# Output projections by Strassen's seven half products, in blocks of 512 tokens, on one Trainium2 core

## The chip, the cores and the metric

The kernel runs as one program on one core of a Trainium2 chip. The metric is the device time of one execution in microseconds (us); the time before is 4362.51 us, the median of 3 runs that lie between 4362.19 and 4364.94 us. Engines are named as in the profile: PE is the matrix engine (PEld its weight loads), DVE the vector engine, ACT the scalar engine, POOL the GpSimd engine, SP the sync engine, which here issues DMAs.

## The reference

Two blocks of a network over 1024 latent tokens of width 1024, with 256 context tokens beside them. The part that the change touches is the projection by which each of three mixers ends. All is in float32.

```python
def mixer(h, hc, ...):                 # first block, one layer
    ...
    y_lat = jnp.concatenate([hy_lat, gla_lat, gdn_lat], axis=-1) @ w_out
    ...
# first_block:  x = x + g1 * y
#               x = x + g2 * sq_relu_mlp(modulate(x, norm2_g[l], sh2, sc2), w_mlp1[l], w_mlp2[l])

def hybrid_layer(x, ctx, ...):         # second block, two layers
    ...
    out_x = jnp.concatenate([att_x, m_x], axis=-1) @ w_out
    x = x + gate_x * out_x
    if not last:
        ...
        out_c = jnp.concatenate([att_c, m_c], axis=-1) @ w_out
        ctx = ctx + gate_c * out_c
    return x, ctx
# between them and at the end: rmsnorm over the width
```

Each `w_out` is 1024 x 1024.

## The kernel before

Activations lie transposed in on-chip memory: the width is split into 8 tiles of 128 partitions, tokens run along the free dimension. Tokens are worked in the blocks of `BLKS` (L17): 512, 512 and, where the context is alive, 256. A plan (`plan`, L4193) yields stages; each stage is an object with a method for each engine, which writes that engine's instructions in order. Nothing reorders them afterwards: an engine's queue is the order of the stages and, within one, the order of its loops. Engines meet by semaphores only: `then_inc` at the producer, `wait_ge` at the consumer; `Stage.begin` (L242) lets an engine wait for all engines' last step of the stage named `after`.

`OutProj` (L2627) is the stage of the change. It stands in the plan three times: "one" (L4244, two blocks), "two0" (L4280, three blocks, the third is the context) and "two1" (the same line, two blocks). In `tensor` (L2645) it goes through the blocks i and in each through the 8 output tiles j. An output tile is 8 float32 matmuls (one for each input tile k) of a 128 x 128 weight against the block's tokens, summed in one of six PSUM banks. The profile counts each float32 matmul as two MATMUL instructions. Weights come in four slots of 256 output columns (`Weights`, L172; `sync`, L2636), each loaded once and used by all blocks. `vector` (L2672) first waits for the whole of x to be back from DRAM, then adds each output tile times its gate to x (L2679). `scalar` (L2663) squares the new x (L555, `Sums.square`), `gpsimd` (L2684) adds the squares up (L565, `Sums.add`) for the norm that follows. x comes back by one DMA that `RestoreX` (L2612) puts on POOL's queue just ahead of `OutProj`; it waits for the end of the stage before.

From block 1 on, each method also issues, behind tile j, a part j of the stage that follows (`post`) for block i-1, so that the norm of block 0 is worked while block 1 is projected. For "one" and "two0" that is `Rms` (L647): PE sums the squares over partitions at j=1 (L572, L574), ACT makes Ln and Exp of it at j=2 (L723, L725), DVE scales (L709) two tiles each at j=3, 4 and 5 and one each at j=6 and 7, and ACT shifts each scaled tile (L729), waiting for it. For "two1" it is `Finish` (L2818): at j=2 to 5 PE transposes 128 tokens into banks 6 and 7 (L2854), and ACT and DVE scale them out of these banks.

Of the kernel before, what the change touches and what calls it, by code (L numbers as in the profile page):

```python
# [9 lines left out]
ALU = mybir.AluOpType  # L10
# [3 lines left out]
T, TC, TT = 1024, 256, 1280  # L14
D = 1024
NEG = -1.0e30
BLKS = [(0, 512), (512, 512), (1024, 256)]  # L17
# [350 lines left out]
class Modulation(Stage):  # L368
# [14 lines left out]
    def steps(self, one, turn):  # L383

        held = None
        for j in self.js:
            one(j)
            if held is not None and self.many:
                turn(held)
            held = j  # L390
            yield
            if not self.many:
                turn(j)
                held = None
            for _ in range(self.gap):
                yield
        if held is not None:
            turn(held)
# [1526 lines left out]
class GlaScan(Stage):  # L1925
# [45 lines left out]
    def four(self, x, t0):  # L1971

        return x[:, :, t0:t0 + 256].rearrange("p a (c t) -> p a c t", c=2)
# [653 lines left out]
class OutProj(Stage):  # L2627

    def __init__(self, K, tag, w, gates, blks, after, sums, post, away=None):
        super().__init__(K, "out_proj", tag, after)
        self.w, self.gates, self.blks, self.sums, self.post, self.away = w, gates, blks, sums, post, away
        self.cat = K.big[:, K.M0:K.M0 + 8 * (TT if len(blks) == 3 or tag != "one" else T)]

    def sync(self, e):  # L2636
        for j in range(0, 8, 2):
            self.K.W.put_cols(e, self.w, 128 * j, 256)

    def steps(self):  # L2640
        for i, (t0, n) in enumerate(self.blks):
            for j in range(8):
                yield i, t0, n, j, (self.tag, "out", j, t0)

    def tensor(self, e):  # L2645
        K, P = self.K, self.sig("tensor")
        self.begin(e)
        pr = Banks(K, range(6))
        cat = self.cat.rearrange("p (a b) -> p a b", a=8)
        ws = []  # L2650
        for i, t0, n, j, u in self.steps():
            if i == 0 and j % 2 == 0:
                ws.append(K.W.use(e, 256))
            used, wv = ws[j // 2]
            b = pr.open(e, u)
            for k in range(8):
                c = 128 * (j % 2)
                t = e.matmul(b[:, 0:n], wv[:, k, c:c + 128], cat[:, k, t0:t0 + n], start=(k == 0), stop=(k == 7))  # L2658
            t.then_inc(P.sem, P.up(("mm", u), used))
            if i:  # L2660
                self.post.tensor_part(e, i - 1, j)

    def scalar(self, e):  # L2663
        S = self.sig("scalar")
        self.begin(e)
        for i, t0, n, j, u in self.steps():
            e.wait_ge(*self.at("free", u, 0))
            self.sums.square(e, S, i, j)
            if i:
                self.post.scalar_part(e, i - 1, j)  # L2670

    def vector(self, e):  # L2672
        K, V = self.K, self.sig("vector")
        self.begin(e)
        e.wait_ge(*self.at("x back", self.tag))
        for i, t0, n, j, u in self.steps():
            x = K.XT[:, j, t0:t0 + n]
            e.wait_ge(*self.at("mm", u))
            e.scalar_tensor_tensor(x, self.bank(u)[:, 0:n], self.gates[1 if t0 >= T else 0][:, j:j + 1], x, ALU.mult,  # L2679
                                   ALU.add).then_inc(V.sem, V.up(("free", u, 0)))  # L2680
            if i:
                self.post.vector_part(e, i - 1, j)

    def gpsimd(self, e):  # L2684
        K, G = self.K, self.sig("gpsimd")
        self.begin(e)
        for i, t0, n, j, u in self.steps():
            self.sums.add(e, G, i, j)
            if i:
                self.post.gpsimd_part(e, i - 1, j)  # L2690
            if self.away is not None and i == len(self.blks) - 1:
                X = self.lane(f"x{j}_away")
                e.wait_ge(*self.at("free", u, 0))
                e.dma_start(K.xs[:, j, :], K.XT[:, j, :]).then_inc(X.sem, X.up(("x away", self.away, j), by=16))


class Mlp(Stage):
# [1495 lines left out]
def plan(K):  # L4193

    A = K.A
    yield Setup(K, "setup", "setup")
    yield Close(K, "setup")
    tmp = K.spare()
    sums = Sums(K, "rms1", K.XT, BLKS, tmp, tmp)
# [7 lines left out]
    m = GdnMem(K)  # L4207
# [6 lines left out]
    m = GlaMem(K)  # L4214
# [8 lines left out]
    m = HyMem(K)  # L4223
# [20 lines left out]
    yield OutProj(K, "one", A["w_out"][0], (K.m6(2), None), BLKS[0:2], "hyena", sums, rms)  # L4244
    yield rms
    yield load
    yield Close(K, "rms2")
# [10 lines left out]
    for l in range(2):  # L4258
        md = K.adac[:, l, :, :]
        m = MlMem(K)  # L4260
# [16 lines left out]
        else:  # L4277
            post = Finish(K, sums, A["final_g_2"])
            yield Fetch(K, post)
        yield OutProj(K, f"two{l}", A["p_out"][l], (md[:, 16:24, 0], md[:, 16:24, 1]), blks, f"at{l}", sums, post,  # L4280
                      "ml1" if l == 0 else None)
        yield post
        yield Close(K, f"rms{5 + l}")

# [96 lines left out]
```

## Time and profile before

| | |
|---|---|
| time, median of 3 | 4362.51 us (4362.19 to 4364.94) |
| span of the profiled execution | 4364.0 us |
| PE busy | 4013.5 us, 92% |
| DVE, ACT, POOL busy | 1530.0, 944.2, 577.8 us |
| mean granted PE clock | 0.949 of full speed |
| DMA | 64 GB/s mean |
| chain that ended last | PE 85%, DVE 7%, issue 3%, ACT 2%, DMA 2%, POOL 1% |
| share of L2658 (the projections' matmuls) in that chain | 8% |

The time of this profiled execution outside its span is not recorded; its span lies 1.5 us above the median of the timed runs. In a row of a line's group, "xcount | busy, mean ns | idle before, releaser" gives how often an instruction ran, its summed time, its mean duration and how long the engine had stood idle before it. Matmuls overlap in the pipeline, so the mean duration of one is longer than its pace; the pace is read from stretches. The granted clock is 1.00 at 2.4 GHz and 0.50 at 1.2 GHz.

### The profile page before, as it was taken

To read this page: it belongs to the slowest core of one execution; us is meant where nothing else is said; L and a number is where in the kernel's file an instruction comes from. 1 tells how busy PE (TensorE), PEld (TensorE's weight loads), DVE (VectorE), ACT (ScalarE), POOL (GpSimd) and SP (SyncE) were. 2 spreads that over 40 slices of the span, in tenths; PEclk is the share of its full clock that TensorE was granted. 3 is DMA by queue.
4 is the path that set the end of the run, shared out by engine and by line. 5 is a ranking of instruction groups with operands and counts; after the bars stand their busy time and mean duration, and the time that the engine had idled before them with its cause. 6 is when DMAs were issued, how large, how long until landed. Compare 5 with 4: busy or idle time off the path is not lost.

```text
span 4364.0 us, 51611 instructions
## 1 busy us (share of the span) xinstructions
PE 4013.5 (92%) x21278; PEld 2527.3 (58%) x21278; DVE 1530.0 (35%) x3530; ACT 944.2 (22%) x1814; POOL 577.8 (13%) x603
## 2 busy tenths in 40 slices
PE   5897997988999999999999897899989998799899
PEld 3477995576467444444444456885554557775454
DVE  2573553235444101111113644531162363621341
ACT  4122331222100200000002411320252310320341
POOL 3002331023000110000002201211000101201001
PEclk7996998988999999999999999999999999999999
DMA  5201002035345111111110312211100312211100
GB/s 189 102 5 26 25 25 88 25 104 180 101 156 203 39 39 39 39 39 39 37 36 28 125 30 73 73 40 51 54 1 25 140 36 57 76 59 39 44 25 39
DMA packets 215480, 278.17 MB, mean 64 GB/s; under 512 B 24333, under 2 KB 174056, under 8 KB 214352
## 3 DMA queue, kind: packets, MB, share of 16 engines
q1 hardware_dynamic: 201904, 206.17, 15.1%
q0 software_dynamic: 13344, 68.70, 4.2%
q8 instruction: 171, 2.80, 0.3%
q14 instruction: 61, 0.50, 0.0%
HBM read 240.03 MB, written 34.81 MB: 63 GB/s over the span
## 4 chain that ended last, share of the span: by engine, by line
PE 85%; DVE 7%; issue 3%; ACT 2%; DMA 2%; POOL 1%; SPq 0%; POOLq 0%; DVEq 0%; ACTq 0%
PE ps L805 16%; PE ps L2748 10%; PE ps L2762 10%; PE ps L2658 8%; PE ps L827 7%; PE ps L3417 6%; PE ps L3699 4%; PE ps L2419 3%; PE ps L3910 2%; PE ps L3893 1%; PE ps L851 1%; DVE big L3512 1%; PE ps L1475 1%; PE ps L1459 1%; DMA big<-hs_scratch 1%
## 5 line engine op out<-in xcount | busy, mean ns | idle before, releaser
L805 PE MATMUL ps<-big 128*128 128x512 f32 (+1 forms) x1760 | 685.6, 551 | 2.8 <-DMA big<-hs_scratch 2.8
L805 PEld LDWEIGHTS ps<-big 128*128 128x128 f32 x1760 | 335.6, 192 | 343.7 <-issue 334.4
L2748 PE MATMUL ps<-big 128*128 128x512 f32 x1024 | 442.3, 594 | 8.6 <-issue 8.6
L2762 PE MATMUL ps<-big 128*128 128x512 f32 x1024 | 440.8, 592 | 0.0
L2812 DVE SCALAR_TENSOR_TENSOR big<-ps,big 128x512 f32<-128x512 f32 x128 | 96.0, 750 | 776.8 <-PE ps L2762 776.8
L2658 PE MATMUL ps<-big 128*128 128x512 f32 (+1 forms) x896 | 359.3, 562 | 3.0 <-DVE big L4028 2.0
L2748 PEld LDWEIGHTS ps<-big 128*128 128x128 f32 x1024 | 195.1, 191 | 254.2 <-issue 254.2
L2762 PEld LDWEIGHTS ps<-big 128*128 128x128 f32 x1024 | 194.6, 190 | 244.9 <-issue 244.9
L827 PE MATMUL ps<-big 128*128 128x256 f32 (+1 forms) x1792 | 319.2, 341 | 12.5 <-DVE big L1909 10.1
L827 PEld LDWEIGHTS ps<-big 128*128 128x128 f32 x1792 | 288.3, 194 | 43.9 <-DVE big L1909 10.3
L2658 PEld LDWEIGHTS ps<-big 128*128 128x128 f32 x896 | 169.6, 190 | 187.6 <-issue 180.8
L3417 PE MATMUL ps<-big 128*128 128x256 f32 x1152 | 251.9, 380 | 5.9 <-DVE big L3590 3.3
L3417 PEld LDWEIGHTS ps<-big 128*128 128x128 f32 x1152 | 217.8, 190 | 36.1 <-issue 6.8
L2779 ACT ACTIVATE big<-ps 128x512 f32<-128x512 f32 x64 | 38.2, 597 | 725.6 <-PE ps L2748 725.6
L932 DVE SCALAR_TENSOR_TENSOR big<-big 128x1024 f32<-128x1024 f32 x130 | 167.0, 1285 | 4.6
L3699 PE MATMUL ps<-big 128*128 128x512 f32 (+1 forms) x416 | 164.7, 552 | 1.9 <-DVE big L3590 1.9
L565 POOL TENSOR_TENSOR big<-big 128x512 f32<-128x512 f32 (+1 forms) x90 | 108.9, 1215 | 403.7 <-ACT big L555 401.5
L2796 POOL TENSOR_TENSOR big<-big 128x512 f32<-128x512 f32 x64 | 66.5, 1039 | 698.0 <-ACT big L2779 698.0
L555 ACT ACTIVATE big<-big 128x512 f32<-128x512 f32 (+1 forms) x120 | 68.7, 595 | 406.3 <-DVE big L2679 310.3
L2679 DVE SCALAR_TENSOR_TENSOR big<-ps,big 128x512 f32<-128x512 f32 (+1 forms) x56 | 39.8, 712 | 311.9 <-PE ps L2658 293.3
L3699 PEld LDWEIGHTS ps<-big 128*128 128x128 f32 x416 | 80.1, 193 | 83.0 <-issue 78.3
L3403 PE MATMUL ps<-big 128*128 128x129 f32 x288 | 63.8, 306 | 69.8 <-DVE big L3526 63.6
(458 smaller groups left out, 5256.4 us busy)
## 6 DMA issues: line engine op xcount, KB each, us to landing
big<-in_w_mlp SPq DMA_DIRECT2D x32, 1024.0 KB, 5.4
big<-in_w_in SPq DMA_DIRECT2D x29, 1024.0 KB, 5.2
big<-in_w_mod SPq DMA_DIRECT2D x24, 1024.0 KB, 5.3
big<-in_w_ada SPq DMA_DIRECT2D x24, 1024.0 KB, 6.3
big<-us_scratch SPq DMA_DIRECT2D x72, 256.0 KB, 4.4
hs_scratch<-big POOLq DMA_DIRECT2D x3, 5120.0 KB, 16.8
big<-c_dft SPq DMA_DIRECT2D x12, 1024.0 KB, 5.7
xs_scratch<-big POOLq DMA_DIRECT2D x16, 640.0 KB, 3.5
```

The lines of the kernel that those rows point to most:

```text
L565: e.tensor_tensor(self.acc[i], self.acc[i], self.sq[q % len(self.sq)][:, 0:n], ALU.add).then_inc(G.sem, G.up(("added", self.tag, q), ("sum ...
L805: t = e.matmul(b[:, 0:n], wv[:, k, 128 * m:128 * m + 128], K.hT[:, k, t0:t0 + n], start=(k == 0), stop=(k == 7))
L827: t = e.matmul(b[:, 0:nn], K.hT[:, k, 128 * i:128 * i + 128], wv[:, k, 0:nn], start=(k == 0), stop=(k == 7))
L932: e.scalar_tensor_tensor(dlat, zlat[:, :, tap:tap + c.seg], c.wcol(m, tap), dlat, ALU.mult, ALU.add).then_inc(V.sem, V.up((self.tag, c.wha ...
L2419: x = e.matmul(b[:, 0:ncol], v[:, t, 128 * k:128 * k + 128], src[:, 4 * half + t, :], start=(t == 0), stop=(t == 3))
L2658: t = e.matmul(b[:, 0:n], wv[:, k, c:c + 128], cat[:, k, t0:t0 + n], start=(k == 0), stop=(k == 7))
L2748: t = e.matmul(b[:, :], wv[:, k, 128 * m:128 * m + 128], K.hT[:, k, t0:t0 + n], start=(k == 0), stop=(k == 7))
L2762: t = e.matmul(b[:, :], wv[:, k, 128 * m:128 * m + 128], h[:, k, t0:t0 + n], start=(k == 0), stop=(k == 3))
L2812: e.scalar_tensor_tensor(x, self.bank(u)[:, :], self.gcol[:, c:c + 1], x, ALU.mult, ALU.add).then_inc(V.sem, V.up(("free", u, 0)))
L3417: x = e.matmul(b[:, 256 * q:256 * q + 256], m.hT[:, k, 128 * t:128 * t + 128], wv[:, k, :], start=(k == 0), stop=(k == 7))
L3699: t = e.matmul(b[:, 0:n], wv[:, k, c:c + 128], K.hT[:, k, t0:t0 + n], start=(k == 0), stop=(k == 7))
L3910: t = e.matmul(self.o[64 * g:64 * g + 64, :], self.m.vtm[:, tiles[k][1], 64 * g:64 * g + 64], tile[g], start=(k == 0), stop=(k == len(tile ...
```

## The change

In `OutProj`, for blocks 0 and 1 (512 tokens), each weight slot (256 output columns, p = 0 to 3) is cut into four quarters W[i][j] (output half i of 128 columns, input half j of four tiles), the block's input into X[j][l] (input half j, token half l of 256 tokens). The direct method makes the 2 x 2 result by eight quarter products; the change makes it by seven, each of 4 float32 matmuls over 256 tokens. For that POOL makes four combinations of the weight quarters for each slot, in block 0, DVE makes four combinations of the input quarters once a block, and intermediate sums are read out of PSUM on the way: DVE adds 7 results of 256 tokens for each slot in place of 2 of 512. Three PSUM results a, b and d are held for each slot; a takes four products one after the other, and before the next is added, DVE must have read it ("P1 out", "P16 out", "P167 out"; for d "P5 out"). One of the weight combinations is written over a weight quarter, so the context block (third block of "two0"), which stays direct (`whole`), has its weights loaded again. The three input combinations that have memory of their own (T1, T2, T4) are shared by the blocks; the fourth is written over the input.

```diff
+    def seven(self, e, P, pr, i, used, wv, p):
+        W, X, (S1, S2, S4), (T1, T2, T4) = self.weights(wv), self.inputs(i), self.S[p], self.T
+        a, b, d = self.unit(i, p)
+        def product(u, w, x, first):
+            o = self.bank(u)[:, 0:256]
+            for k in range(4):
+                t = e.matmul(o, w[:, k, :], x[:, k, :], start=(first and k == 0), stop=(k == 3),
+                             skip_group_check=not first)
+            return t
+        pr.open(e, a)
+        product(a, W[0][0], X[0][0], True).then_inc(P.sem, P.up(("P1", a)))
+        pr.open(e, b)
+        product(b, W[0][1], X[1][0], True).then_inc(P.sem, P.up(("mm", b)))
+        e.wait_ge(*self.at(self.tag, "weight sum", p, 2))
+        e.wait_ge(*self.at(self.tag, "input sum", i, 2))
+        e.wait_ge(*self.at("P1 out", a))
+        product(a, S2, T2, False).then_inc(P.sem, P.up(("P16", a)))
+        pr.open(e, d)
+        product(d, S1, T1, True).then_inc(P.sem, P.up(("P5", d)))
+        e.wait_ge(*self.at(self.tag, "weight sum", p, 3))
+        e.wait_ge(*self.at(self.tag, "input sum", i, 3))
+        e.wait_ge(*self.at("P16 out", a))
+        product(a, W[1][0], X[0][1], False).then_inc(P.sem, P.up(("P167", a)))
+        e.wait_ge(*self.at(self.tag, "weight sum", p, 4))
+        e.wait_ge(*self.at("P5 out", d))
+        product(d, S4, X[1][1], False).then_inc(P.sem, P.up(("mm", d)))
+        e.wait_ge(*self.at(self.tag, "input sum", i, 4))
+        e.wait_ge(*self.at("P167 out", a))
+        product(a, W[1][1], T4, False).then_inc(P.sem, P.up(("mm", a), used, (self.tag, "block", i)))
     def tensor(self, e):
...
+        for i in range(len(self.blks)):
+            for p in range(4):
+                if i != 1:
+                    ws.append(K.W.use(e, 256))
+                (self.whole if i == 2 else self.seven)(e, P, pr, i, *ws[4 * (i == 2) + p], p)
+                if i:
+                    for j in (2 * p, 2 * p + 1):
+                        self.post.tensor_part(e, i - 1, j)
     def scalar(self, e):
...
+        for i in range(len(self.blks)):
+            for j in range(8):
+                e.wait_ge(*self.at(self.tag, "x", i, j))
+                self.sums.square(e, S, i, j)
+                if i:
+                    self.post.scalar_part(e, i - 1, j)
+    def input_sums(self, e, V, i):
+        X, (T1, T2, T4) = self.inputs(i), self.T
+        if i:
+            e.wait_ge(*self.at(self.tag, "block", i - 1))
+        e.tensor_tensor(T1, X[0][1], X[0][0], ALU.subtract).then_inc(V.sem, V.up())
+        e.wait_ge(V.sem, V.n)
+        e.tensor_tensor(T2, X[1][1], T1, ALU.subtract).then_inc(V.sem, V.up((self.tag, "input sum", i, 2)))
...
     def vector(self, e):
...
+        for i, (t0, n) in enumerate(self.blks):
+            if i < 2:
+                self.input_sums(e, V, i)
+            if i == 0:
+                e.wait_ge(*self.at("x back", self.tag))
+            for p in range(4):
...
+                    add(i, a, ("P1", a), j, t0, 256, ("P1 out", a))
+                    add(i, b, ("mm", b), j, t0, 256, ("free", b, 0))
+                    add(i, a, ("P16", a), j, t0 + 256, 256, ("P16 out", a))
+                    add(i, d, ("P5", d), j + 1, t0 + 256, 256, ("P5 out", d))
+                    add(i, a, ("P167", a), j + 1, t0 + 256, 256, ("P167 out", a))
+                    add(i, d, ("mm", d), j, t0 + 256, 256, ("free", d, 0), (self.tag, "x", i, j))
+                    add(i, a, ("mm", a), j + 1, t0, 256, ("free", a, 0), (self.tag, "x", i, j + 1))
+                if i:
+                    for x in (j, j + 1):
+                        self.post.vector_part(e, i - 1, x)
+    def weight_sums(self, e, G, p):
...
+        e.tensor_tensor(S1, W[1][0], W[1][1], ALU.add).then_inc(G.sem, G.up())
+        e.wait_ge(G.sem, G.n)
+        e.tensor_tensor(S2, S1, W[0][0], ALU.subtract).then_inc(G.sem, G.up((self.tag, "weight sum", p, 2)))
+        e.tensor_tensor(W[1][0], W[0][0], W[1][0], ALU.subtract).then_inc(
+            G.sem, G.up((self.tag, "weight sum", p, 3)))
+        e.wait_ge(*self.at(self.tag, "weight sum", p, 2))
+        e.tensor_tensor(S4, W[0][1], S2, ALU.subtract).then_inc(G.sem, G.up((self.tag, "weight sum", p, 4)))
     def gpsimd(self, e):
...
+        for i in range(len(self.blks)):
+            for j in range(8):
+                if i == 0 and j % 2 == 0:
+                    self.weight_sums(e, G, j // 2)
+                self.sums.add(e, G, i, j)
```

`Sums.add` does nothing for j = 0 and 7; for the others it waits for the square of tile j.

## Rows read from the trace of the kernel before

**Rows 1.** The page: busy time of the engines, and the group of L2658.
```profile
PE 4013.5 (92%) x21278; PEld 2527.3 (58%) x21278; DVE 1530.0 (35%) x3530; ACT 944.2 (22%) x1814; POOL 577.8 (13%) x603
...
L2658 PE MATMUL ps<-big 128*128 128x512 f32 (+1 forms) x896 | 359.3, 562 | 3.0 <-DVE big L4028 2.0
```
**Rows 2.** The chain that ended last: start us, us, what.
```profile
1391.97 68.91 PE ps L2658 x160
...
3310.97 68.91 PE ps L2658 x160
...
3431.42 20.73 PE ps L2658 x96
...
4232.77 68.91 PE ps L2658 x160
```
**Rows 3.** Timeline of DVE, the first add of each stage (start us, us).
```profile
1406.15 1.41 DVE L2679 SCALAR_TENSOR_TENSOR big<-ps,big 128x512 f32<-128x512 f32 x2 [16.62 <-PE ps L2658]
...
3320.54 0.75 DVE L2679 SCALAR_TENSOR_TENSOR big<-ps,big 128x512 f32<-128x512 f32 x1 [9.78 <-DMA big<-xs_scratch]
...
4241.26 0.75 DVE L2679 SCALAR_TENSOR_TENSOR big<-ps,big 128x512 f32<-128x512 f32 x1 [8.70 <-DMA big<-xs_scratch]
```
**Rows 4.** L2679 by duration (ns min/median/max), and three groups of DVE by form.
```profile
L2679 DVE SCALAR_TENSOR_TENSOR big<-ps,big x56: 483/750/752, 1406.2 to 4348.2; 128x512 f32<-128x512 f32 x48, 128x256 f32<-128x256 f32 x8
...
L932 DVE SCALAR_TENSOR_TENSOR big<-big 128x1024 f32<-128x1024 f32 x130 | 167.0, 1285 | 4.6
...
L709 DVE SCALAR_TENSOR_TENSOR big<-big 128x512 f32<-128x512 f32 x64 | 50.0, 832 | 20.6 <-ACT big L725 20.6
...
L3748 DVE TENSOR_TENSOR big<-big 128x512 f32<-128x512 f32 x20 | 13.9, 693 | 14.5 <-POOL big L3667 14.5
```
**Rows 5.** Timelines of ACT and POOL, start of stage "one": square, then add.
```profile
1413.64 0.63 ACT L555 ACTIVATE big<-big 128x512 f32<-128x512 f32 x1 [5.42 <-DVE big L2679]
...
1414.35 1.26 POOL L565 TENSOR_TENSOR big<-big 128x512 f32<-128x512 f32 x1 [4.70 <-ACT big L555]
```
**Rows 6.** POOL's sums of two tiles: min/median/max ns of L565 and L2796.
```profile
L565 POOL TENSOR_TENSOR big<-big x90: 713/1266/1723, 28.4 to 4342.8; 128x512 f32<-128x512 f32 x72, 128x256 f32<-128x256 f32 x18
...
L2796 POOL TENSOR_TENSOR big<-big x64: 1038/1039/1040, 1526.3 to 2288.4; 128x512 f32<-128x512 f32 x64
```
**Rows 7.** Timeline of ACT and DVE in block 1 of stage "one".
```profile
1470.94 1.28 ACT L723 ACT_TABLE_LOAD   x1
...
1474.23 0.63 ACT L725 ACTIVATE big<-big 128x512 f32<-128x512 f32 x1
...
1483.90 1.41 DVE L709 SCALAR_TENSOR_TENSOR big<-big 128x512 f32<-128x512 f32 x2
```
**Rows 8.** Timeline of PE behind three stretches of idleness.
```profile
1516.77 28.45 PE L2748 MATMUL ps<-big 128*128 128x512 f32 x62 [8.60 <-issue]
...
2405.71 2.08 PE L572 MATMUL ps<-big 128*128 128x512 f32 x2 [4.73 <-ACT big L734]
...
2950.01 15.67 PE L3699 MATMUL ps<-big 128*128 128x512 f32 x32 [0.94 <-DVE big L3590]
```
**Rows 9.** Windows behind them: stretch, busy of each engine, PEclk, DMA, GB/s.
```profile
1519.00:1520.00 1.00, 1.00 (x2) 0.34 (x1) 0.00 (x0) 0.17 (x2) 0.72 (x1) 0.50 0.00 0
...
2410.00:2411.00 1.00, 1.00 (x3) 0.39 (x2) 0.29 (x1) 0.00 (x0) 0.00 (x0) 0.55 0.00 0
...
2952.00:2953.00 1.00, 1.00 (x2) 0.34 (x2) 0.00 (x0) 0.00 (x0) 0.80 (x3) 0.50 0.50 168
```
**Rows 10.** Timeline of PE in stage "two1", block 1: transposes for `Finish`.
```profile
4310.17 1.04 PE L2854 MATMUL ps<-big 128*128 128x128 f32 x8
```
**Rows 11.** Timelines at the end of stages "one" and "two0": ACT and PE.
```profile
1505.28 0.72 ACT L729 ACTIVATE big<-big 128x512 f32<-128x512 f32 x1
...
1505.31 1.12 PE L574 MATMUL ps<-big 128*128 128x512 f32 x2 [0.65 <-ACT big L555]
...
3453.16 0.70 PE L574 MATMUL ps<-big 128*128 128x256 f32 x2 [0.59 <-ACT big L555]
```

More of the change, by code:

```diff
@@ L2636, in sync, with weights @@
     def sync(self, e):
[L2637 to L2643, printed above, removed]
+        for _ in range(len(self.blks) - 1):
+            for j in range(0, 8, 2):
+                self.K.W.put_cols(e, self.w, 128 * j, 256)
+    def weights(self, wv):
+        return [[wv[:, 4 * j:4 * j + 4, 128 * i:128 * i + 128] for j in range(2)] for i in range(2)]
@@ new lines, in inputs, with places, four @@
+    def inputs(self, i):
+        t0 = self.blks[i][0]
+        return [[self.cat[:, 4 * j:4 * j + 4, t0 + 256 * l:t0 + 256 * l + 256] for l in range(2)] for j in range(2)]
+    @staticmethod
+    def places(K, mem, last):
+        def four(x):
+            return x.rearrange("p (k c) -> p k c", k=4)
+        T, S = [mem.get(4, 256) for _ in range(2)], [four(K.columns().get(512)), four(mem.get(512))]
+        if last:
+            S += [four(K.R1[:, 4096 + 512 * i:4608 + 512 * i]) for i in range(8)]
+            return T + [mem.get(4, 256)], S + [four(mem.get(512)), four(K.R1[:, 9224:9736])]
+        S += [four(K.hT0[:, k, 512:1024]) for k in range(8)]
+        S += [K.hT0[:, 4:8, 1024 + 128 * j:1152 + 128 * j] for j in range(2)]
+        return T + [K.hT0[:, 0:4, 1024:1280]], S
@@ new lines, in unit, with whole @@
+    def unit(self, i, p):
+        return [(self.tag, "out", i, p, x) for x in "abd"]
+    def whole(self, e, P, pr, i, used, wv, p):
+        t0, n = self.blks[i]
+        for m in range(2):
+            u = (self.tag, "out", i, 2 * p + m)
+            b = pr.open(e, u)
+            for k in range(8):
+                t = e.matmul(b[:, 0:n], wv[:, k, 128 * m:128 * m + 128], self.cat[:, k, t0:t0 + n], start=(k == 0),
+                             stop=(k == 7))
+            t.then_inc(P.sem, P.up(("mm", u), used))
@@ L2648, in tensor @@
         pr = Banks(K, range(6))
[L2649 to L2661, printed above, removed]
+        self.base, ws = K.W.uses, []
+        for i in range(len(self.blks)):
[6 more added lines that the diff above has]
+                        self.post.tensor_part(e, i - 1, j)
     def scalar(self, e):
@@ new lines, in vector @@
+        for i, (t0, n) in enumerate(self.blks):
[4 more added lines that the diff above has]
+            for p in range(4):
+                j = 2 * p
+                if i == 2:
+                    for m in range(2):
+                        u = (self.tag, "out", i, j + m)
+                        add(i, u, ("mm", u), j + m, t0, n, ("free", u, 0), (self.tag, "x", i, j + m))
+                else:
+                    a, b, d = self.unit(i, p)
+                    add(i, a, ("P1", a), j, t0, 256, ("P1 out", a))
[8 more added lines that the diff above has]
+                        self.post.vector_part(e, i - 1, x)
@@ L2686, in gpsimd @@
         self.begin(e)
[L2687 to L2694, printed above, removed]
+        for i in range(len(self.blks)):
[3 more added lines that the diff above has]
+                self.sums.add(e, G, i, j)
+                if i:
+                    self.post.gpsimd_part(e, i - 1, j)
+                if self.away is not None and i == len(self.blks) - 1:
+                    X = self.lane(f"x{j}_away")
+                    e.wait_ge(*self.at(self.tag, "x", i, j))
+                    e.dma_start(K.xs[:, j, :], K.XT[:, j, :]).then_inc(X.sem, X.up(("x away", self.away, j), by=16))
 class Mlp(Stage):
@@ L4243, in plan @@
     rms = Rms(K, "rms2", K.XT, K.hT0, BLKS[0:2], [(sums, i) for i in range(2)], tmp, cols, begun=1)
-    yield OutProj(K, "one", A["w_out"][0], (K.m6(2), None), BLKS[0:2], "hyena", sums, rms)
+    mem = OutProj.places(K, tmp, 0)
+    yield OutProj(K, "one", A["w_out"][0], (K.m6(2), None), BLKS[0:2], "hyena", sums, rms, mem)
     yield rms
```

31 lines of the change are left out of this document (17 added, 14 removed).

## The prediction

> **What bounds the kernel now.** I read the page first: PE is busy 92% of the span, and the projections' matmuls (L2658) are 359.3 us of it, with 3.0 us of idleness ahead of them in all [rows 1]. Then the chain that ended last: in each of the three stages it is PE alone, 160 MATMULs in 68.91 us without a break [rows 2]. So PE's pace is the stage's time, nothing else shows, and a saved matmul is a gain as long as nothing new makes PE wait. The pace is 68.91 / 160 = 430.7 ns for 512 columns and 20.73 / 96 = 215.9 ns for 256 columns, each with its own weights [rows 2]: half the columns cost almost exactly half, so the smaller products lose nothing by themselves. Last I read what the other engines do in these stages, since the change makes PE wait for them inside each slot: today six banks keep PE apart from them, and DVE's first add comes 14.18, 9.57 and 8.49 us after the stage's first matmul (first row of each stage in [rows 2] against [rows 3]) without PE noticing.
>
> **What is removed.** A weight slot ("pair" of output tiles) in a block of 512 is now 32 MATMULs of 512 columns, 32 x 0.4307 = 13.78 us. After: 7 products x 4 x 2 = 56 of 256 columns, 56 x 0.2159 = 12.09 us. That is 1.69 us for each of 24 pairs (four pairs, two blocks, three stages), 40.6 us in all. The context block keeps its matmuls; its second load of 4 MB follows slots that come free a block earlier, and I cost it at nothing: three pairs of context, 3/4 x 20.73 = 15.5 us of PE, hide even the last slot [rows 2].
>
> **What is added: waits of PE.** The first two products need nothing; they end 3.45 us into the pair. The third needs the weight sum S2, the input sum T2 and "P1 out", DVE's add of the first product. The five products from there on take 8.64 us. So a pair costs 8.64 us plus the time at which the last of the three is there, at least 3.45. DVE's add of 256 columns is 0.48 us [rows 4]. Later waits in the pair each have a whole product (8 x 0.2159 = 1.73 us) for one add and hold nobody up.
>
> *Block 0, first pair.* DVE waits for all of x before "P1 out", so it is there at 14.18, 9.57 and 8.49 us plus 0.48: 14.66, 10.05, 8.97. Behind that wait stand all of DVE's adds, and now PE. The four input sums stand ahead of it and are hidden by it (about 5 us, below). The pairs take 23.3, 18.7 and 17.6 us in place of 13.78: +9.5, +4.9, +3.8, together **+18.2**.
>
> *The clock.* PE now stands idle 11.2, 6.6 and 5.5 us there. In the trace, after 8.60 us of idleness 62 MATMULs took 28.45 us in place of 26.7 and the granted clock was still 0.50 at 1519; after 4.73 us it was 0.55 in the window at 2410, 5 us after the restart at 2405.71; behind light work with short gaps 32 MATMULs took 15.67 us in place of 13.78 [rows 8, 9]. The losses are 1.75, about 2.6 and 1.9 us. I take 1.9 three times, **+5.7**; bounds 0 to 2.6 each.
>
> *Block 0, pairs 2 to 4.* POOL comes to the weight sums of a pair only behind the sum of squares of the last tile but one of the pair before (L565), since `gpsimd` is written so. From the end E of a pair: DVE's add until 0.52 (0.04 to start), the square 0.63 from there (1.17), POOL starts 0.08 later [rows 5] and does the square's sum, S1 and S2, three instructions of 1.26 us [rows 5, 6]: S2 at E + 5.03, pair 13.67 us, -0.11 for each of nine pairs, **-1.0**. The gain of these pairs is eaten by POOL. The weight sums' own form is not in the trace: bounds are 1.04 us (L2796) and 1.72 us (the longest L565, beside DVE work on SBUF); I take 1.26, the median of the form nearest to it [rows 6].
>
> *Block 1, first pair.* T1, T2 and T4 are shared with block 0, so DVE starts the four input sums only when block 0's last product is done, and its own add of that product and the add of P1 lie around them. A sum of 128 x 1024 from SBUF is not in the trace: twice 0.693 less one start-up as the lower bound, 1.285 (L932) as the upper one [rows 4]; I take 1.24. P1 out at 0.52 + 4 x 1.24 + 0.48 = 5.96, pair 14.6 us: +0.86 three times, **+2.6**.
> The Trainium skill (VectorE: DVE Perf Modes, the cycle table with its errata) gives a float32 sum of two tensors (N + 151) / 0.96 ns, an estimate of 1.22 us here; the whole sum would change by 0.3 us.
>
> *Block 1, pair 2.* Nothing new: -1.69 three times, **-5.1**.
>
> *Block 1, pairs 3 and 4 under `Rms`.* The parts for both tiles now stand behind all seven adds. In pair 2 ACT makes Ln and Exp with their table loads, 1470.94 to 1474.86, 3.9 us [rows 7]; it starts behind the square of tile 2, whose last product ends 1.73 before E and whose add ends at E - 1.21, so at E - 0.55, and is done at E + 3.4. DVE then scales two tiles (1.41 us, [rows 7]) and only then reads P1: 3.4 + 1.41 + 0.48 = 5.3, pair 13.9: +0.16. In the next pair DVE has four tiles to scale, 0.70 to 0.83 us each [rows 4, 7], I take 3.1 us: 0.52 + 3.1 + 0.48 = 4.1, pair 12.74: -1.04. For two stages: **-1.8**.
>
> *Block 1, pairs 3 and 4 in "two1".* `Finish` has PE transpose twice behind a pair, each 8 MATMULs, 1.04 us in all [rows 10], into the same two banks; the second now has no tile of matmuls between and waits for ACT and DVE (0.75 us) to empty them, some 0.45 us. Two times -1.69 + 0.45: **-2.5**.
>
> *Ends.* The last square stood 0.8 us behind the last matmul. Now ACT's shift of tile 6 is ahead of it in ACT's queue, and that waits for DVE's scaling of tile 6, which stands behind the last add: add until 0.52, scaling until 1.25, shift (0.72) until 2.0, square until 2.65, against 1.5 at which L574 starts today [rows 11]. **+1.2** in "one", +1.3 in "two0" (its L574 follows 1.2 behind), -0.3 in "two1", which has no such part: together **+2.2**.
>
> **The sum.** 18.2 + 5.7 - 1.0 + 2.6 - 5.1 - 1.8 - 2.5 + 2.2 = +18.3 us. Said the other way: a gross gain of 40.6 against 59 us of new waits, 23.3 of them for x, 5.7 of clock, 30 for sums, norms and ends. On the profiled span 4364.0 + 18.3 = 4382.3; what lies around the span is not touched, and the median of the runs stands 1.5 us lower: **4381 us**.
>
> **Rivals.** *A, cheap waits.* POOL's three instructions run at 1.04 us, as L2796 does with both inputs the same, and the clock stays up in "two0" and "two1": 9 x 0.66 + 3.8 = 9.7 us less, 4371. Against it: L565 has two inputs and a median of 1.27 us [rows 6].
> *B, contention and clock.* POOL's weight sums run at 1.72 beside DVE, 9 x 2 x 0.45 = +8, and every second of the twelve short stops of 1.6 to 2.5 us lets the clock fall as the stretch at 2950 did (1.9 us [rows 8, 9]), +11: 4389 to 4400. For it: that stretch had no stop longer than 2 us. Against it: PE works at full load between the stops here.
> The Trainium skill (TensorE: Matmul & The Clock Gate, "A second HAM failure mode: psum-queue depth-cycling") says that small idle times between groups of matmuls alone can make the clock go up and down; it speaks for this rival, and against the change.
> *C, faster.* Only the wait for x is left as a stop. Its place is the third product of each pair: if from the second pair on S2 and P1 out are there by 3.45 us, POOL's chain of 5.03 us would have to shrink by 1.6 and DVE would have to be free of sums and scalings by then. Then the gain is 40.6 - 23.3 - 5.7 = 11.6, 4351 us. It decides in favour of the change as soon as the 30 us behind the first pairs fall under 11.6. No row shows POOL or DVE at such a pace.
> *D, the seven products don't run in 7/8 of the time.* Each wait splits PE's stream into groups of 8 MATMULs, and where PE really stops, one MATMUL's pace (0.22 us) may be lost to the weight load that can't be hidden: 21 stops, up to +4, 4385.
>
> **Chances.** Forecast 0.60; A 0.14; B 0.15; C 0.05; D 0.06. The range leaves out C and the far end of B: **4367 to 4396**. A change of 0.2% (8.7 us, 4353.8 to 4371.2) is about what a measurement of this kernel can tell from none. Faster than that: C, 0.05. Within it: half of A and the low tail of the forecast, 0.13. Slower: 0.82.
>
> **What would show it.** Right: in the changed kernel's timeline PE stands still about 11, 6.6 and 5.5 us after the first 16 MATMULs of each stage (two products), released by DVE's add behind the DMA of x; in block 0 each later pair has a stop of about 1.6 us released by POOL; block 1 begins with one of 2.5 us behind DVE's sums; the stages take about 10, 6 and 2 us longer than now. Wrong: block 0's later pairs at 12.1 us (POOL not in the way), or a granted clock of 1.00 through the first stops, or clock losses in later pairs.

## Result: 37 us slower, twice the forecast

The changed kernel takes 4399.93 us, the median of 4 runs (4394.66 to 4402.63), against 4362.66 us before (4 runs now, one more than ahead of the prediction, 4362.19 to 4364.94); the ratio is 1.008, 95% interval 1.0066 to 1.0094. The forecast was 4381 us in a range of 4367 to 4396. The sign and the places of the stops were right, the size was not: +37 us in place of +18.

The page of the changed kernel, its busy times and the groups of the projections' matmuls and adds (L2692 takes the place of L2658 of [rows 1], L2762 that of L2679):

```profile
span 4400.3 us, 53232 instructions
PE 3996.0 (91%) x21854; PEld 2645.7 (60%) x21854; DVE 1615.5 (37%) x3674; ACT 941.9 (21%) x1814; POOL 641.6 (15%) x651
...
L2692 PE MATMUL ps<-big 128*128 128x256 f32 x1344 | 310.3, 393 | 56.0 <-DVE big L2762 37.8
...
L2762 DVE SCALAR_TENSOR_TENSOR big<-ps,big 128x256 f32<-128x256 f32 x176 | 85.1, 484 | 251.4 <-PE ps L2692 222.6
```

PE is busy 17.5 us less than before and the span is 36.3 us longer: saved work shows, though less than the 40.6 us of the forecast (the clock, below, takes part of it back), and 56.0 us of idleness now lie ahead of L2692, where L2658 had 3.0 [rows 1]. The timeline of PE through stage "one" shows the whole story (start us, us, and in brackets the idle time ahead and who ended it); before, [rows 2] had one stretch of 68.91 us here:

```profile
1390.73 3.69 PE L2692 MATMUL ps<-big 128*128 128x256 f32 x16 [0.98 <-ACT big L2505]
1405.41 14.20 PE L2692 MATMUL ps<-big 128*128 128x256 f32 x56 [10.99 <-DVE big L2762]
1421.30 12.35 PE L2692 MATMUL ps<-big 128*128 128x256 f32 x56 [1.69 <-POOL big L2796]
1435.35 12.35 PE L2692 MATMUL ps<-big 128*128 128x256 f32 x56 [1.70 <-POOL big L2796]
1449.40 12.35 PE L2692 MATMUL ps<-big 128*128 128x256 f32 x56 [1.69 <-POOL big L2796]
1464.46 11.93 PE L2692 MATMUL ps<-big 128*128 128x256 f32 x40 [2.70 <-DVE big L2762]
1476.22 1.02 PE L572 MATMUL ps<-big 128*128 128x512 f32 x2
1477.08 1.02 PE L574 MATMUL ps<-big 128*128 128x512 f32 x2
1477.94 15.70 PE L2692 MATMUL ps<-big 128*128 128x256 f32 x72
1496.66 14.01 PE L2692 MATMUL ps<-big 128*128 128x256 f32 x56 [3.02 <-DVE big L2762]
1511.10 8.87 PE L2692 MATMUL ps<-big 128*128 128x256 f32 x40 [0.43 <-DVE big L2762]
1520.92 1.10 PE L572 MATMUL ps<-big 128*128 128x512 f32 x2 [0.95 <-POOL big L565]
1522.65 1.12 PE L574 MATMUL ps<-big 128*128 128x512 f32 x2 [0.64 <-ACT big L555]
```

An undisturbed group of 56 takes 12.35 us, one of 40 takes 8.87. So three rows are too long at the same work: 14.20, 11.93 and 14.01 (warm, below, has 12.32 in the place of the last). They follow the stops of 10.99, 2.70 and 3.02 us, and the windows of the changed kernel show why (stretch, length, busy of PE, PEld, DVE, ACT, POOL, granted clock, DMA share, GB/s):

```profile
1406.00:1408.00 2.00, 2.00 (x6) 1.64 (x5) 0.00 (x0) 0.00 (x0) 0.00 (x0) 0.50 0.15 59
...
1468.00:1470.00 2.00, 2.00 (x6) 1.64 (x5) 0.48 (x1) 0.00 (x0) 0.00 (x0) 0.50 0.00 0
...
1498.00:1500.00 2.00, 2.00 (x6) 1.56 (x6) 0.48 (x1) 0.00 (x0) 0.00 (x0) 0.50 0.00 0
```

PE is fully busy in all three and runs at half its clock, 1.2 GHz. The forecast had the first of them, not the other two. The stop of 2.70 us stands in all three stages, and a slow row doesn't follow it each time. In "two0" and "two1":

```profile
3399.92 8.87 PE L2692 MATMUL ps<-big 128*128 128x256 f32 x40 [2.70 <-DVE big L2762]
...
4331.29 10.43 PE L2692 MATMUL ps<-big 128*128 128x256 f32 x40 [2.70 <-DVE big L2762]
```

I measure each stage from its first matmul to the start of the first row that ends it (L574, and in "two1" the first matmul of the mean, L2845 before and L2966 after). By the PE timelines, with 1391.97 and 1505.31 of [rows 2, 11] as an example of before:

| profiled execution | "one" | "two0" | "two1" | sum | rest of the span |
|---|---|---|---|---|---|
| before | 113.3 | 142.2 | 117.0 | 372.5 | 3991.5 |
| changed | 131.9 | 153.0 | 123.3 | 408.3 | 3992.1 |

35.7 of the 36.3 us lie in the three stages. This table is the measure for the experiments, since the rest of the span moves between 3987 and 3995 us from run to run with no edit there.

### The profile page after: what moved, and what is told of

Its sections match the earlier page's. It is cut to its first block, busy times and chain, and to the rows that moved or that the text cites. A ratio compares the mean times of both kernels' runs of the same rounds, so it can differ in the third digit from the quotient of the medians.

```text
span 4400.3 us, 53232 instructions
## 1 busy us (share of the span) xinstructions
PE 3996.0 (91%) x21854; PEld 2645.7 (60%) x21854; DVE 1615.5 (37%) x3674; ACT 941.9 (21%) x1814; POOL 641.6 (15%) x651
## 4 chain that ended last, share of the span: by engine, by line
PE 82%; DVE 8%; issue 4%; ACT 2%; DMA 2%; POOL 2%; SPq 0%; POOLq 0%; DVEq 0%; ACTq 0%
PE ps L805 15%; PE ps L2869 10%; PE ps L2883 10%; PE ps L827 7%; PE ps L3538 6%; PE ps L2692 5%; PE ps L3820 4%; PE ps L2419 3%; PE ps L4031 1%; PE ps L851 1%; PE ps L4014 1%; DVE big L3633 1%; PE ps L1475 1%; PE ps L1459 1%; DMA big<-hs_scratch 1%
## 5 line engine op out<-in xcount | busy, mean ns | idle before, releaser
L805 PE MATMUL ps<-big 128*128 128x512 f32 (+1 forms) x1760 | 684.7, 550 | 3.1 <-DMA big<-hs_scratch 3.1
L805 PEld LDWEIGHTS ps<-big 128*128 128x128 f32 x1760 | 335.2, 192 | 343.4 <-issue 334.1
L2692 PE MATMUL ps<-big 128*128 128x256 f32 x1344 | 310.3, 393 | 56.0 <-DVE big L2762 37.8
L2869 PEld LDWEIGHTS ps<-big 128*128 128x128 f32 x1024 | 195.4, 191 | 254.6 <-issue 254.6
L2883 PEld LDWEIGHTS ps<-big 128*128 128x128 f32 x1024 | 194.6, 190 | 244.9 <-issue 244.9
L2692 PEld LDWEIGHTS ps<-big 128*128 128x128 f32 x1344 | 263.2, 197 | 102.3 <-issue 42.4
L827 PEld LDWEIGHTS ps<-big 128*128 128x128 f32 x1792 | 288.3, 194 | 43.9 <-DVE big L1909 10.3
L3538 PE MATMUL ps<-big 128*128 128x256 f32 x1152 | 251.9, 380 | 7.0 <-DMA big<-hs_scratch 3.6
L3538 PEld LDWEIGHTS ps<-big 128*128 128x128 f32 x1152 | 217.8, 190 | 37.2 <-issue 7.9
L2762 DVE SCALAR_TENSOR_TENSOR big<-ps,big 128x256 f32<-128x256 f32 x176 | 85.1, 484 | 251.4 <-PE ps L2692 222.6
L3820 PE MATMUL ps<-big 128*128 128x512 f32 (+1 forms) x416 | 164.7, 552 | 1.9 <-DVE big L3711 1.9
L565 POOL TENSOR_TENSOR big<-big 128x512 f32<-128x512 f32 (+1 forms) x90 | 106.6, 1190 | 381.5 <-ACT big L555 379.4
L3820 PEld LDWEIGHTS ps<-big 128*128 128x128 f32 x416 | 80.1, 193 | 83.0 <-issue 78.3
```

What stands on the lines that cost most here:

```text
L565: e.tensor_tensor(self.acc[i], self.acc[i], self.sq[q % len(self.sq)][:, 0:n], ALU.add).then_inc(G.sem, G.up(("added", self.tag, q), ("sum ...
L805: t = e.matmul(b[:, 0:n], wv[:, k, 128 * m:128 * m + 128], K.hT[:, k, t0:t0 + n], start=(k == 0), stop=(k == 7))
L827: t = e.matmul(b[:, 0:nn], K.hT[:, k, 128 * i:128 * i + 128], wv[:, k, 0:nn], start=(k == 0), stop=(k == 7))
L2692: t = e.matmul(o, w[:, k, :], x[:, k, :], start=(first and k == 0), stop=(k == 3), skip_group_check=not first)
L2869: t = e.matmul(b[:, :], wv[:, k, 128 * m:128 * m + 128], K.hT[:, k, t0:t0 + n], start=(k == 0), stop=(k == 7))
L2883: t = e.matmul(b[:, :], wv[:, k, 128 * m:128 * m + 128], h[:, k, t0:t0 + n], start=(k == 0), stop=(k == 3))
```

## The experiments

Theory 1 is the prediction's account with the clock losses that the trace adds: each product saves what the pace says, and all of the loss is PE standing, plus the slow clock behind it. The rivals are that the narrower, grouped products are slow by themselves, that a removed wait uncovers another of the same length, and that the lost time behind a stop isn't the clock.

### seven_free: are the products themselves worth 40 us?

```diff
-        e.wait_ge(*self.at("P1 out", a))
-        product(a, S2, T2, False).then_inc(P.sem, P.up(("P16", a)))
+        product(a, W[1][0], X[0][1], False)
...
-            if i < 2:
-                self.input_sums(e, V, i)
...
-                    add(i, a, ("P1", a), j, t0, 256, ("P1 out", a))
...
-                if i == 0 and j % 2 == 0:
-                    self.weight_sums(e, G, j // 2)
```

DVE's other reads of sums that aren't finished go as well.

> The seven products of each pair run on the plain quarters, with no sums of weights or inputs and no reading of PSUM in between; DVE adds only the finished results, so the values computed are not the reference's. Theory 1 (the products save what the pace says, all the loss is waits): 24 pairs of 12.09 us in place of 13.78, less 1 to 2 us at the ends of two stages, 4322 to 4325 us. Rival (groups of eight narrow MATMULs run slower than 7/8 of the time, as my prediction's rival D): 4330 us or more.

4330.01 us (4324.69 to 4334.5), ratio 0.9918 (0.9898 to 0.9939) to a kernel before that took 4361.22 us beside it: -31 us. The interval of the ratio, 0.9898 to 0.9939, is -44 to -27 us and holds theory 1's -39 to -36 as well as the rival's -31, so the median doesn't decide. The timeline of PE does (stage "one"):

```profile
1391.29 60.67 PE L2692 MATMUL ps<-big 128*128 128x256 f32 x280 [0.97 <-ACT big L2505]
...
1453.51 36.42 PE L2692 MATMUL ps<-big 128*128 128x256 f32 x168
```

60.67 / 280 = 216.7 ns and 36.42 / 168 = 216.8 ns, with the last matmul's tail in it, no stop inside: the pace of [rows 2] holds in groups of eight. The stages are 101.7, 130.3 and 105.6, together 34.9 us shorter than before. So most of the gross gain of 40.6 us is real. The missing 5.7 us can be followed from the start of each pair to the start of the next: before, most pairs take 13.73 us, not the forecast's 13.78, and now 12.09, so each of the 24 saves 1.65 us in place of 1.69 (1.1 us in all); the ends cost 1.6, 1.3 and 0.3 us; and in "two1" the transposes, now twice in a row behind a pair, cost 0.73 us two times.

### sums_ahead: POOL's order in block 0

```diff
-                if i == 0 and j % 2 == 0:
-                    self.weight_sums(e, G, j // 2)
+                if i == 0 and j == 0:
+                    for p in range(4):
+                        self.weight_sums(e, G, p)
```

> The changed kernel with all sixteen weight sums put ahead of POOL's first sum of squares. Theory 1: the nine stops of 1.69 us (pitch 14.05 us, where 12.1 is PE's own) are POOL's order alone and vanish, -17.6 us, about 4382 us; PE then runs pairs 2 to 4 of block 0 without a stop. Rival (behind POOL stands DVE's add of the first product, which would stop PE nearly as long): less than -6 us, 4394 or more.

4376.39 us (4364.27 to 4380.22), ratio 1.0029 (1.0017 to 1.0042). PE in stage "one":

```profile
1391.94 3.69 PE L2692 MATMUL ps<-big 128*128 128x256 f32 x16 [0.99 <-ACT big L2505]
1406.83 50.46 PE L2692 MATMUL ps<-big 128*128 128x256 f32 x224 [11.19 <-DVE big L2762]
1459.98 8.87 PE L2692 MATMUL ps<-big 128*128 128x256 f32 x40 [2.70 <-DVE big L2762]
```

All nine stops are gone and nothing took their place: 17.6 us by theory 1. The stages are 21.7 us shorter than in the changed kernel. Most of the other 4.1 us is the clock: the 40 MATMULs behind the stop of 2.70 now take 8.87 us in all three stages, where the changed kernel had 11.93, 8.87 and 10.43, 4.6 us more; some tenths of that go again behind the first stops. The median is 5.6 us under theory 1's 4382, which had counted on the stops alone.

### p1_early: the stop at the start of block 1

```diff
+    def input_sums_2(self, e, V, i):
+        X, (T1, T2, T4) = self.inputs(i), self.T
         e.tensor_tensor(X[0][1], X[1][1], X[0][1], ALU.subtract).then_inc(
             V.sem, V.up((self.tag, "input sum", i, 3)))
...
                     add(i, a, ("P1", a), j, t0, 256, ("P1 out", a))
                     add(i, b, ("mm", b), j, t0, 256, ("free", b, 0))
+                    if i == 1 and p == 0:
+                        self.input_sums_2(e, V, i)
```

> The changed kernel, in block 1 with DVE's adds of the first two products put between the second and the third input sum, so that PE can go on after two sums instead of four. Theory 1: the stop at the start of block 1 falls from 2.7 us to at most 0.5, -7 to -8 us; if the clock losses behind that stop (3.1, 0 and 1.6 us in the profiled run) hang on it, another -4 to -5, together about 4387 us. Rival (the clock falls there for the stops before it): -7 us only, about 4393, with windows at clock 0.50 still there.

4386.92 us (4376.98 to 4396.93), ratio 1.0056 (1.0037 to 1.0075). In all three stages the stop is 0.42 to 0.43 us and the 40 MATMULs behind it take 8.87. The stages sum to 396.8, 11.4 us shorter than the changed kernel: 3 x 2.27 of stops, 4.6 of clock, as theory 1 had it (about 4387). The stops of 1.69 us are all still there, so they alone don't make the clock fall.

### warm: is the time behind a stop the clock?

```diff
+        many = {(0, 0): {"one": 24, "two0": 13, "two1": 12}[self.tag], (1, 0): 6,
+                (1, 2): 0 if self.tag == "two1" else 6}.get((i, p), 0)
+        if many:
+            o = Banks(self.K, (7,)).open(e, (self.tag, "warm", i, p), 0)[:, 0:256]
+            for k in range(many):
+                e.matmul(o, W[0][1][:, k % 4, :], X[1][0][:, k % 4, :], start=True, stop=True)
         e.wait_ge(*self.at(self.tag, "weight sum", p, 2))
         e.wait_ge(*self.at(self.tag, "input sum", i, 2))
         e.wait_ge(*self.at("P1 out", a))
```

> The changed kernel with idle matmuls in PE's stops: extra products into a bank that nobody reads, as long as the stop (24, 13 and 12 float32 matmuls at the first stop of the three stages, 6 each at the stop that opens block 1 and at the one of 3.0 us behind its second pair). Clock theory (the losses behind stops, 6.1 us at the first stops and 8.1 at later ones, are the clock that fell while PE stood): -10 to -14 us, 4386 to 4390, granted clock 1.00 through all three stages. Rival (the time behind a stop is lost by refilling or by the waiting itself): 4400 or more.

4384.47 us (4381.6 to 4398.89), ratio 1.0055 (1.0036 to 1.0074), against 1.008 for the changed kernel: 11 us (by the ratios) to 15 us (by the medians) come back by adding useless work. The median lies 1.5 us under the clock theory's 4386 to 4390 and far from the rival's 4400. PE, stage "one" (L2705 are the extra matmuls), and two windows:

```profile
1395.03 10.52 PE L2705 MATMUL ps<-big 128*128 128x256 f32 x48
1406.30 12.32 PE L2692 MATMUL ps<-big 128*128 128x256 f32 x56 [0.74 <-DVE big L2768]
...
1460.61 2.75 PE L2705 MATMUL ps<-big 128*128 128x256 f32 x12
1463.47 8.87 PE L2692 MATMUL ps<-big 128*128 128x256 f32 x40
```

```profile
1391.00:1417.00 26.00, 24.75 (x114) 21.54 (x115) 10.25 (x12) 1.67 (x3) 9.20 (x8) 1.00 0.63 235
...
1463.00:1470.00 7.00, 6.89 (x32) 5.81 (x31) 2.25 (x5) 0.00 (x0) 0.00 (x0) 1.00 0.02 4
```

14.20 us became 12.32, 11.93 became 8.87 and 14.01 became 12.32, at a granted clock of 1.00, with DVE's release of PE as late as before (14.79 us into the stage, 14.68 in the changed kernel). In "two0" and "two1" too every group behind a filled stop takes 12.32 or 8.87 us, so the time behind the stops is the clock. The stages sum to 395.3, 13.0 us less than the changed kernel, against 13.8 us of rows that were too long (5.8 at the first stops, 4.6 and 3.4 later); in "two0" the wait for x was 0.8 us longer in this run (10.79 us in place of 9.97).

### no_x: what stands behind the wait for x?

```diff
         X = self.lane("x_back")
+        if self.name == "restore":
+            X.keep(("x back", self.tag))
+            return
         e.dma_start(K.XT[:, self.k0:, 0:self.n], ...)
...
-            if i == 0:
+            if i == 0 and self.tag != "one":
                 e.wait_ge(*self.at("x back", self.tag))
```

> The changed kernel without the DMA that brings x back for the three projections; they add to what stands in that memory, so the values are not the reference's. If the wait for x costs what its stop shows, 23 us and 6 us of clock go, 4371 us. Theory 1 says that another wait stands right behind it: DVE's four input sums come ahead of its add of the first product and hold PE some 2.7 to 3 us in each stage, so -14 to -15 us of stops, and -2 to -6 of clock: 4379 to 4384 us, with the first stop of each stage 2.5 to 3.5 us long and released by DVE.

4391.47 us (4382.86 to 4394.09), ratio 1.0063 (1.0049 to 1.0076). The first stops are 5.21, 4.74 and 4.79 us, not 2.5 to 3.5, and the clock falls behind them as before (13.82, 15.38 and 14.75 us for 56). Of the 22.8 us of first stops 14.7 still stand without any x, and only 8.2 us came off the stages. DVE's sums at the start of "two0", and POOL's beside them:

```profile
3321.59 1.22 DVE L2749 TENSOR_TENSOR big<-big 128x1024 f32<-128x1024 f32 x1 [0.20 <-DVE big L4152]
3322.85 2.18 DVE L2751 TENSOR_TENSOR big<-big 128x1024 f32<-128x1024 f32 x1
3324.95 2.11 DVE L2752 TENSOR_TENSOR big<-big 128x1024 f32<-128x1024 f32 x1
3326.99 2.28 DVE L2755 TENSOR_TENSOR big<-big 128x1024 f32<-128x1024 f32 x1
```

```profile
3321.75 2.20 POOL L2797 TENSOR_TENSOR big<-big 128x512 f32<-128x512 f32 x1 [175.05 <-DVE big L4152]
3324.02 1.95 POOL L2799 TENSOR_TENSOR big<-big 128x512 f32<-128x512 f32 x1
```

A sum of 1024 columns takes 1.22 us alone and 2.1 to 2.3 beside POOL's, and POOL's four take 1.95 to 2.25 in place of 1.26. So theory 1's direction holds (another wait stands there), my size for it didn't: the two engines slow each other down. The Trainium skill (GPSIMD Engine Reference, 8. Key points) says that GpSimd shares its memory interfaces with VectorE and that instructions of VectorE with two inputs from SBUF contend; this run agrees.

### scale_late: the stop of 3.02 us

```diff
                     add(i, b, ("mm", b), j, t0, 256, ("free", b, 0))
+                    if i == 1 and later:
+                        for x in later:
+                            self.post.vector_part(e, i - 1, x)
+                        later = []
                     add(i, a, ("P16", a), j, t0 + 256, 256, ("P16 out", a))
...
+                if i == 1 and p in (1, 2) and self.tag != "two1":
+                    later = [j, j + 1]
```

> The changed kernel, in stages one and two0, block 1, with DVE's scaling parts of pairs 2 and 3 issued behind the adds of the next pair's first two products instead of ahead of them. Theory 1: the stop of 3.02 us with its clock loss of 1.8 us, and the one of 0.43, go in both stages, -10 to -12 us, 4388 to 4390 us. Rival (the scaling only stands in the way of the next add, P16 out, and the stop moves there): less than -5 us, 4395 or more.

4391.49 us (4387.86 to 4394.98), ratio 1.0066 (1.0052 to 1.008). That is short of theory 1's 4388 to 4390 and better than the rival's 4395, so the timed runs alone don't decide; the trace does. The stages "one" and "two0" are 6.5 and 5.2 us shorter than in the changed kernel, 11.6 us together, of which 1.6 us is other luck with the clock at the stop of 2.70 in "one" (10.29 us behind it in place of 11.93). PE runs 144 MATMULs there in 31.43 us without a stop; one of 0.26 us is left.

### first_direct, ordered, tuned: all edits at once

In first_direct the first pair of block 0 is direct, so that PE has 13.8 us of work for which DVE needn't have x, and the three edits above are in:

```diff
+    def direct(self, i, p):
+        return i == 2 or (i, p) == (0, 0)
...
+                if i == 0 and j == 0:
+                    for p in (1, 2, 3):
+                        self.weight_sums(e, G, p)
+                if i == 0 and j == 4:
+                    e.wait_ge(*self.at("mm", (self.tag, "out", 0, 1)))
+                    self.weight_sums(e, G, 0)
```

> Four edits on the changed kernel: the first pair of block 0 in the direct way (it needs no DVE before PE goes on), POOL's sums for the other pairs put ahead, input sums 3 and 4 behind the adds of the first two products, scaling parts late. Theory 1 (the loss is these waits and nothing else): 21 of 24 pairs keep 1.69 us, -35.5 us on the kernel before, +2.5 at the ends and 1 to 3 of short stops: 4328 to 4333 us. Rival (the stops are pushed to other places, as DVE has seven adds a pair to do in order): 4345 or more, still around the kernel before.

4342.1 us (4335.63 to 4343.51), ratio 0.9948 (0.9933 to 0.9963): faster than the kernel before, by 21 us. That lies outside theory 1's 4328 to 4333, and under the rival's 4345. The stages sum to 347.8, 24.7 us under the kernel before. Of the 35.5 us, 10.8 are lost: stops of 0.81, 0.34 and 1.02 us in block 0, 0.43 in block 1, 0.26 behind the scaling, each with some 0.26 us that a restart and a matmul's tail cost at a stop, the ends, and the pairs of transposes in "two1".

> first_direct, and in block 1 the scaling of tiles 6 and 7 moved into the last pair, in the context block each part behind its own tile again, so that the last square doesn't wait for a scaling. Theory 1: 1.2 us each come back in two stages, 4326 to 4331 us, and L574 starts 1.5 and 1.2 us behind the last matmul as before the change. Rival: the ends were not held by that, same as first_direct.

In ordered, `vector_part` of tiles 6 and 7 was put behind `later` in the last pair, ahead of "P16 out", and the context block got its old order. 4345.24 us (4336.5 to 4347.56), ratio 0.9956 (0.9943 to 0.9968): no better. The ends did what was expected, L574 of "two0" waits 0.59 us again as in [rows 11], in place of 1.86. But six scalings in a row ahead of one add took DVE 5.07 us and PE got a new stop, with a slow clock behind it:

```profile
1486.91 5.07 DVE L709 SCALAR_TENSOR_TENSOR big<-big 128x512 f32<-128x512 f32 x6
```

```profile
1492.52 7.11 PE L2695 MATMUL ps<-big 128*128 128x256 f32 x24 [2.59 <-DVE big L2768]
```

24 MATMULs take 5.42 us undisturbed (scale_late), so 1.7 us are the clock's. tuned spreads the parts in that pair:

```diff
+                    behind = later[:1] if p == 3 else later
+                    for x in behind:
+                        self.post.vector_part(e, i - 1, x)
+                    later = later[len(behind):]
                     add(i, a, ("P16", a), j, t0 + 256, 256, ("P16 out", a))
+                    for x in later:
+                        self.post.vector_part(e, i - 1, x)
...
+                    if i == 1 and p == 3 and self.tag != "two1":
+                        self.post.vector_part(e, i - 1, j)
                     add(i, a, ("P167", a), j + 1, t0 + 256, 256, ("P167 out", a))
...
+                    if i == 1 and p == 3 and self.tag != "two1":
+                        self.post.vector_part(e, i - 1, j + 1)
```

> The kernel ordered had all six scaling parts of block 1's last pair ahead of one add and got a stop of 2.6 us there in two stages, while its ends came back as wanted. Here the parts are spread in that pair, at most two ahead of any add. Theory 1: both stops go with what follows them (1.6 us of slow clock each), the ends stay: the three stages together 345 us or a little less, against 347.8 in first_direct and 372.5 before the change, 4334 to 4340 us. Rival (any scaling between the adds stops PE for its length): no better than first_direct's 4342.

4338.03 us (4334.03 to 4346.65), ratio 0.9952 (0.9938 to 0.9965) to 4361.4 us, inside theory 1's 4334 to 4340. Stages 104.1, 132.1 and 108.6, sum 344.8. Block 1 of "one" behind its first pair is one stretch:

```profile
1458.15 36.61 PE L2695 MATMUL ps<-big 128*128 128x256 f32 x168
```

The trace puts it 3.0 us under first_direct; the intervals of the timed runs overlap, so between these two only the trace decides. Both beat the kernel before.

## Why the prediction was right in sign and wrong in size

In the order of its steps; measured values are from the PE timelines of both kernels' three stages, each pair from its first matmul to the next pair's, with the slow clock taken out into rows of its own.

| step | forecast | measured |
|---|---|---|
| first pair of block 0, wait for x | +18.2 | +18.6 |
| clock behind these stops | +5.7 | +5.8 |
| block 0, pairs 2 to 4 | -1.0 | +2.8 |
| block 1, first pair | +2.6 | +3.9 |
| block 1, pair 2 | -5.1 | -5.0 |
| pairs 3 and 4 under `Rms` | -1.8 | +1.3 |
| pairs 3 and 4 in "two1" | -2.5 | -1.8 |
| ends | +2.2 | +2.2 |
| clock behind later stops | 0 | +8.0 |
| sum | +18.3 | +35.7 |

The rows are rounded; the sum is the stages' own difference. That a pair saves 1.65 us and not 1.69 (seven_free) is in every row of pairs.

**Right.** The pace, the wait for x with its three lengths (restarts at 14.68, 9.97 and 9.17 us, forecast 14.66, 10.05 and 8.97), POOL's chain as the releaser of every stop in block 0, the stop of block 1, the ends. That the context's second load costs nothing: in "two0" its 32 and 96 MATMULs run at the old pace (20.88 us for 96 in the timeline, with the last one's tail).

**The step that failed: "The clock".** I let it fall behind the three first stops only and counted 0 for the shorter ones, with no more against it than that PE works at full load between them; it cost 8.0 us there, the largest part of the 17.4 us by which the sum is short, and with it the forecast would have been 4389, 11 us under the measured median. Rival B had it for short stops, at 0.15, as one lump for all twelve stops of 1.6 to 2.5 us and together with slow weight sums, which weren't there in block 0's later pairs (L2796's median is 1.26 us). The runs separate the stops by length and by what stood ahead of them. Behind 1.69 us, nine times in each of five kernels (changed, p1_early, warm, no_x, scale_late), the 56 MATMULs always take 12.35 us: never a loss. Behind 2.70 us, where stops of 1.69 come ahead (changed, no_x, scale_late), 6 of 9 lose 1.4 to 3.1 us; where none comes ahead (sums_ahead), 0 of 3. Behind 2.59 (ordered) 2 of 2, behind 3.02 (changed, sums_ahead, p1_early, no_x) 8 of 8, at 1.4 to 1.7 us. In the changed kernel four gaps, two of "one" and one each of "two0" and "two1", were forecast at 0 and cost 3.1, 1.7, 1.7 and 1.6 us. That these losses hang on the stops is shown by the edits: p1_early shortened the one stop, scale_late took away the other, warm filled both, and each time the matmuls behind ran at the undisturbed pace.
The Trainium skill (TensorE: Matmul & The Clock Gate, "A second HAM failure mode: psum-queue depth-cycling") lets small idle times between groups of matmuls make the clock go up and down. Here that holds for 16 of the 22 stops of 2.6 to 3.0 us and for none of the 45 of 1.69.

**Terms with the right mechanism and a wrong size.** *Pairs 2 to 4 of block 0*: 14.05 us in place of 13.67. The chain of stage "one", in order of time (start us, us, what):

```profile
1405.41 10.76 PE ps L2692 x40
1416.20 0.50 DVE big L2762
1416.71 0.64 ACT big L555
1417.42 1.27 POOL big L565
1418.69 1.23 POOL big L2794
1419.99 1.27 POOL big L2796
1421.30 8.91 PE ps L2692 x40
1430.24 0.50 DVE big L2762
```

The steps are those that I added up, each of nearly its size. What I left out is that 40 MATMULs end 8.91 us after they begin, not 8.64. Of these 0.27 us, 0.10 go at the restart: the first MATMUL behind the stop starts together with its own weight load, and the next one follows after 0.32 us, not 0.22. The other 0.17 are the last one's tail: a MATMUL takes 0.38 us and the pace hides 0.17 of it as long as another follows. With some 0.1 us of hops that is 0.38, nine times 3.4 us; the other 0.4 us is the smaller saving. *Block 1, first pair*: again 0.27 us at the stop, and T1 slowed by POOL's last sum (1.45 us in place of 1.22 in "one"). *Pairs 3 and 4*: again the stops' own cost, and DVE's two scalings took 2.43 us in place of 1.41, one of them beside POOL's L565:

```profile
1493.70 2.43 DVE L709 SCALAR_TENSOR_TENSOR big<-big 128x512 f32<-128x512 f32 x2 [2.98 <-ACT big L725]
...
1494.19 1.38 POOL L565 TENSOR_TENSOR big<-big 128x512 f32<-128x512 f32 x1 [3.20 <-ACT big L555]
```

**Hidden, and wrong all the same.** I took the four input sums at the start for about 5 us and covered by the wait for x. They are covered, but take 6.8, 7.7 and 8.4 us in the three stages of the changed kernel, and in "two1" DVE's first add starts only 0.2 us behind them. So the price that I put on x, 23.3 us, is for the most part not x's alone: no_x got 8.2 us back.

**The rivals.** A (cheap waits) fell: POOL's sums in block 0's later pairs took 1.26 us, not 1.04, and the clock fell in all three stages. Of D, slow products fell by seven_free's pace, but its mechanism at a stop was there: the first MATMUL behind each of the changed kernel's 19 stops holds the next one back by 0.08 to 0.10 us at full clock, some 2 us in all where D had up to 4. The profile shows the weight load starting with that MATMUL; no run tells whether it is the cause. C (faster) was for the most part a matter of the order: its condition, S2 and "P1 out" there by 3.45 us, is nearly met by first_direct and tuned, at the cost of one pair's 1.69 us in each stage; it gave -21 to -23 us, since there the wait for x is gone as well.

**Still open.** Why the clock fell in 6 of 9 stops of 2.70 us and not in the other three can't be told from these runs, nor whether the three of sums_ahead stayed fast for want of stops ahead of them or by chance. Between the products no run has a stop longer than 1.70 and shorter than 2.59 us, so where the losses begin is not shown.

## What to carry to other kernels

An algorithm that saves matmuls but reads partial results on the way ties PE to the slowest queue at its side: before counting the saved products, write down for each wait what stands ahead of the releasing instruction in its own queue, and spread or reorder that first. Here the seven products cost 37 us in one order of the other engines' work and gained 23 in another, with one pair in eight left direct. In this kernel a stop of PE of 2.6 to 3.0 us cost its length, 0.3 us of restart and tail, and in 16 of 22 cases 1.4 to 3.1 us of slow clock, mostly 1.7.

## What the runs showed of the hardware that I had not expected

- The granted clock fell to 0.50 behind stops as short as 2.59 us in a stream that was otherwise full, and one such stop (2.70 us) cost 3.1 us behind it, more than its own length. Useless matmuls in the stops gave 13.0 us back in the stages.
- A sum of two SBUF tensors on DVE (1.22 us for 128 x 1024) and one on POOL (1.26 us for 128 x 512) slow each other when they run side by side: DVE's took 2.1 to 2.9 us, POOL's mostly 1.95 to 2.25 (changed kernel and no_x). The worst row that the trace of before had shown was 1.72 us on POOL [rows 6].
